# A dense expert layer: 128 instead of 112 tokens scattered through DRAM, 32 instead of 36 lots of one-hot products, another place for two exponentials and for the zeroing of the scratch

## The reference

```python
def peer(h, w_q, sub_keys, u_tab, v_tab):          # h: 256 tokens, width 1024
        q = (xc @ w_q).reshape(T, PEER_HEADS, 2, PEER_QDIM // 2)
        s = jnp.einsum('thcd,hcnd->thcn', q, sub_keys)       # 8 heads x 2 halves x 128 keys
        sv, si = lax.top_k(s, PEER_TOPK)                     # 16 of 128
        comb = (sv[:, :, 0, :, None] + sv[:, :, 1, None, :]).reshape(T, PEER_HEADS, 256)
        cv, ci = lax.top_k(comb, PEER_TOPK)
        eidx = i1 * PEER_NKEYS + i2                          # one of 128 * 128 experts
        w = jax.nn.softmax(cv, axis=-1)
        a = jax.nn.gelu(jnp.einsum('td,thkd->thk', xc, u_tab[eidx])) * w
        return jnp.einsum('thk,thkd->td', a, v_tab[eidx])
```

## Time and profile before

| | |
|---|---|
| median of 3 runs | 2952.64 us (2947.97 to 2952.76) |
| the profiled execution | 2951.89 us, of which the span is 2950.2 us |
| PE busy | 2817.8 us, 96% of the span |
| DVE / ACT / POOL busy | 1989.1 / 1482.9 / 489.1 us |
| chain that ended last | PE 90%, DVE 4%, ACT 3%, DMA 2%, issue 1% |
| granted TensorE clock | 0.982 of full speed on average |
| indirect DMAs (L800) | 256, 420.1 us busy on POOL, mean 1641 ns |

### The profile page before, as it was taken

How to read it: one execution, slowest core, us unless ns; L and a number is a source line. 1 busy time by engine, 2 the same in 40 slices (tenths; PEclk the granted TensorE clock), 3 DMA queues, 4 the chain that set the end, 5 groups by cost and what they waited for, 6 DMA issues and landing times.

```text
span 2950.2 us, 51661 instructions
## 1 busy us (share of the span) xinstructions
PE 2817.8 (96%) x17556; PEld 2517.7 (85%) x17556; DVE 1989.1 (67%) x3725; ACT 1482.9 (50%) x2397; POOL 489.1 (17%) x390
## 2 busy tenths in 40 slices
PE   8889998999999989999999999999899999999998
PEld 6679887788789889999988888785899999988886
DVE  4557975679965759866866666516479848766666
ACT  2444454544443444667855555205245668745554
POOL 0000100011100000477700000000000787400000
PEclk9999999999999999999999999989999999999999
DMA  8638973489854445666556666540355775566663
GB/s 283 209 116 260 346 252 112 128 243 355 331 171 129 143 143 177 176 174 157 137 178 215 214 215 213 126 143 15 93 176 178 178 174 135 145 212 216 215 213 131
DMA packets 355204, 547.85 MB, mean 186 GB/s; under 512 B 71073, under 2 KB 251681, under 8 KB 354466
## 3 DMA queue, kind: packets, MB, share of 16 engines
q1 hardware_dynamic: 303618, 471.46, 50.3%
q0 software_dynamic: 51488, 75.11, 9.8%
HBM read 545.33 MB, written 15.84 MB: 190 GB/s over the span
## 4 chain that ended last, share of the span: by engine, by line
PE 90%; DVE 4%; ACT 3%; DMA 2%; issue 1%; ACTq 0%; SPq 0%; DVEq 0%
PE ps L1002 34%; PE ps L929 12%; PE ps L933 12%; PE ps L930 12%; PE ps L980 4%; PE ps L1369 2%; DMA tile_ring<-mlp_w_in 1%; PE ps L1490 1%; PE ps L904 1%; PE ps L1132 1%; PE ps L863 1%; PE ps L1579 1%; PE ps L874 1%; PE ps L964 1%; PE ps L1030 1%
## 5 line engine op out<-in xcount | busy, mean ns | idle before, releaser
L929 PE MATMUL ps<-x_high,w_high 128*128 128x256 f32 x3264 | 819.2, 288 | 28.5 <-DVE x_low L2730 10.6
L930 PE MATMUL ps<-x_low,w_high 128*128 128x256 f32 x3264 | 805.1, 284 | 0.0
L929 PEld LDWEIGHTS ps<-x_high,w_high 128*128 128x128 f32 x3264 | 628.5, 193 | 41.3 <-issue 26.0
L800 POOL DMA_INDIRECT by_key<-spare x256 | 420.1, 1641 | 1330.3 <-DVE spare L2805 1216.0
L930 PEld LDWEIGHTS ps<-x_low,w_high 128*128 128x128 f32 x3264 | 629.8, 193 | 0.4
L2231 DVE TENSOR_TENSOR w_low<-tile_ring,w_high 128x1024 fp32r<-128x1024 f32 x256 | 313.8, 1226 | 249.4 <-ACT w_high L1821 249.4
L933 PE MATMUL ps<-x_high,w_low 128*128 128x256 f32 x3264 | 460.8, 284 | 1.4 <-DVE w_low L3026 1.4
L1821 ACT ACTIVATE w_high<-tile_ring 128x1024 fp32r<-128x1024 f32 x256 | 271.5, 1061 | 346.0 <-PE ps L1002 346.0
L933 PEld LDWEIGHTS ps<-x_high,w_low 128*128 128x128 f32 x3264 | 423.9, 193 | 1.6 <-DVE w_low L3026 1.6
L1002 PE MATMUL ps<-w_high,x_high 128*128 128x512 f32 x1440 | 389.9, 393 | 21.2 <-DVE x_low L2186 16.7
L1964 ACT ACTIVATE w_high<-tile_ring 128x1024 fp32r<-128x1024 f32 x256 | 270.7, 1058 | 262.9 <-PE ps L933 215.5
(11 more groups left out here) (365 smaller groups left out, 3253.2 us busy)
## 6 DMA issues: line engine op xcount, KB each, us to landing
tile_ring<-peer_u SPq DMA_DIRECT2D x256, 512.0 KB
tile_ring<-peer_v SPq DMA_DIRECT2D x256, 512.0 KB
arena<-mod_w POOLq DMA_DIRECT2D x112, 512.0 KB, 6.4
tile_ring<-mlp_w_in SPq DMA_DIRECT2D x64, 512.0 KB
tile_ring<-mlp_w_out SPq DMA_DIRECT2D x64, 512.0 KB
tile_ring<-ret_w_in SPq DMA_DIRECT2D x48, 512.0 KB
tile_ring<-peer_w_q SPq DMA_DIRECT2D x32, 512.0 KB
by_key<-zero_rows POOLq DMA_DIRECT2D x16, 896.0 KB, 5.1
```

The costliest lines, as they stand in the source:

```text
L800: pool.indirect_dma_start(out=flat, out_offset=bass.IndirectOffsetOnAxis(ap=slot_at[0:SCATTER, n:n + 1], axis=0), in_=slot_weight[0:SCATTE ...
L929: nc.tensor.matmul(dst, cols, x_high[:, c, :], start=c == 0, stop=False)
L930: nc.tensor.matmul(dst, cols, x_low[:, c, :], start=False, stop=False)
```

## The change

- `SCATTER` becomes 128: the whole first block of tokens goes by the indirect DMAs, which then have 128 elements each; the scratch grows from 128 x 128 x 112 to 128 x 128 x 128 floats. The second block goes as 32 lots, after the tiles 92 to 123. Only the second block's routing is turned (three records), and DVE lifts it in one piece.
- The exponentials move from 36 and 68 tiles to 32 and 64, and from between two loops into four pairs that are written out: they now stand behind the first `high` of these four and ahead of its gelu.
- The zeroing of layer 0's scratch moves behind the modulation loads and `ret_const`, and layer 1's behind layer 0's scatters; each has 8 DMAs of 1 MB instead of 896 KB, each waited for as before.
- DVE drops one product of 128 x 128 in the first block's `finish`.

```diff
-SCATTER = 112
+SCATTER = P
-RAISED_AT = (36, 68)
+RAISED_AT = (32, 64)
...
-                        ("cross1", 4), ("mlp1", 16), ("retention", 8), ("gates", 8), ("route0", 18),
-                        ("weigh0", LOTS), ("nsa", 20), ("route1", 18), ("weigh1", LOTS)):
+                        ("cross1", 4), ("mlp1", 16), ("retention", 8), ("gates", 8), ("route0", 17),
+                        ("weigh0", LOTS), ("nsa", 20), ("route1", 17), ("weigh1", LOTS)):
...
-            n_clear = 0
-            for l in range(DEPTH):
-                for i in range(P // CLEAR):
-                    pool.dma_start(by_key[l][:, i * CLEAR:(i + 1) * CLEAR, :],
-                                   I["zero_rows"].rearrange("p (i t) -> p i t", t=SCATTER)).then_inc(cleared, 16)
-                    n_clear += 16
-                    pool.wait_ge(cleared, n_clear)
...
-            landed = 0
+            n_clear, landed = 0, 0
+
+            def clear(l):
+                nonlocal n_clear
+                for i in range(P // CLEAR):
+                    pool.dma_start(by_key[l][:, i * CLEAR:(i + 1) * CLEAR, :],
+                                   I["zero_rows"].rearrange("p (i t) -> p i t", t=SCATTER)).then_inc(cleared, 16)
+                    n_clear += 16
+                    pool.wait_ge(cleared, n_clear)
+            clear(0)
...
+                if l + 1 < DEPTH:
+                    clear(l + 1)
...
-                for b in range(TB):
-                    u = open_unit()
-                    for k in range(3):
-                        mm = nc.tensor.transpose(bank(u)[:, k * P:(k + 1) * P], route[:, b, k, :], ident)
-                    mm.then_inc(unit_done, 1)
+                u = open_unit()
+                for k in range(3):
+                    mm = nc.tensor.transpose(bank(u)[:, k * P:(k + 1) * P], route[:, 1, k, :], ident)
+                mm.then_inc(unit_done, 1)
...
-                def tiles(j):
+                def tiles(j, raise_block=None):
                     for k in range(RING):
                         high(k + 2, j)
+                        if k == 0 and raise_block:
+                            raise_block()
                         gelu(k, j)
...
-                    act.wait_ge(routed, TB * l + b + 1)
-                    A(route[:, b, 2, :], route[:, b, 2, :], ACT.Exp).then_inc(pick_exp, 1)
-                    j0 = RAISED_AT[b] // RING
+
+                    def raise_block():
+                        act.wait_ge(routed, TB * l + b + 1)
+                        A(route[:, b, 2, :], route[:, b, 2, :], ACT.Exp).then_inc(pick_exp, 1)
+                    tiles(RAISED_AT[b] // RING, raise_block)
+                    j0 = RAISED_AT[b] // RING + 1
...
-                    ins = V.tensor_tensor(own, own, wide, ALU.mult)
-                    if b == 1:
-                        operand(ins)
+                    else:
+                        operand(V.tensor_tensor(own, own, wide, ALU.mult))
...
-                    z = bank(u)[:, 0:3 * P].rearrange("p (k t) -> p k t", t=P)[:, :, 0 if i else SCATTER:P]
-                    own = slice(P - SCATTER, own_tokens) if i else slice(0, P - SCATTER)
-                    V.tensor_scalar(minus[:, :, own], z[:, 0:3:2, :], -1.0, None, ALU.mult).then_inc(dve_step, 1)
+                    z = bank(u)[:, 0:3 * P].rearrange("p (k t) -> p k t", t=P)
+                    V.tensor_scalar(minus, z[:, 0:3:2, :], -1.0, None, ALU.mult).then_inc(dve_step, 1)
                     settle()
-                    return V.tensor_copy(slots[:, :, own], z)
-                take(2, lift_slots)
+                    return V.tensor_copy(slots, z)
+                take(1, lift_slots)
```

More of the change, by code:

```diff
@@ L694, in peer @@
                 bare.up(P)
-                units.up(2 + LOTS)
+                units.up(1 + LOTS)
                 panels_next()
```

## The result

The median of six runs is 2963.17 us (2958.1 to 2965.31), against 2950.99 us for the kernel before (six runs, 2947.07 to 2952.76). The ratio is 1.004, 95% interval 1.0027 to 1.0053. The forecast was 2939.7 us; its range ended at 2947.5. The profiled execution has a span of 2963.6 us, 13.4 more than before.

The account below looks back on a forecast made before the run. PE bounds the kernel, with 90% of the chain. Fewer lots -7.1, turned routing -0.7, table loads -6.3, stall +0.9 and zeroing +1.0 give -12.2 us: from 2951.89 to 2939.7 us, range 2935.5 to 2947.5.

Parts of the forecast that it names:

- the scatters' duration: POOL's 256 scatters: 128 elements for 112 add 159 ns each, 20.4 us over a layer's 128, just hidden.
- the rivals with late scatters: Scatters a little late, 2946.1 us, up to 2948, chance 0.12; or slower than the kernel before, chance 0.04.
- the scatters set the end of peer_u: SP's wait: above 0.28 us extra per scatter, two layers lose over 18.1 us, kernel slower by 0.2%; chance 0.04.
- 128e - 26.8: Loss per layer in us where positive, for extra time e per scatter: nothing at 159 ns, 3.2 us at 234.
- The slack: Time before SP needs layer 0's scatters: 22.3 us spare against 20.4 added, with POOL starting at about 1201.5.
- the sum: All terms over the kernel: -7.1 - 0.7 - 6.3 + 0.9 + 1.0 = -12.2 us.
- Lots and turned routing: Peer layers: four fewer lots each gain 7.1 us on PE, three fewer turned records gain 0.7 us.
- Table loads in the loops: ACT's gelu table reloads in later peer_u loop rounds go: 3.17 us a layer, 6.3 us gained.
- The stall at the exponential: PE's wait at each exponential grows by 0.22 us, four times: 0.9 us lost; one distance near 4.8 at each.
- Zeroing: Scratch clearing moved beside tile loads slows products by 1.3%: 1.0 us lost in all, bounds 0 to 6.
- just hidden: Scatters' added 20.4 us a layer fit in 22.3 us of spare time before SP waits, so nothing is lost.

Follow-up runs that it names:

- e1: The changed kernel with 112 instead of 128 elements in each scatter, tokens 112 to 127 getting no weights: 2938.79 us, ratio 0.9964.
- e4: The changed kernel with SCATTER back at 112 (36 lots, six turned records), exponentials and zeroing as changed: 2946.76 us, ratio 0.9986.
- e3: The kernel before with only the exponentials moved, to 32 and 64 tiles in written-out pairs, ahead of gelu: 2948.40 us, ratio 0.9991.
- e7: The changed kernel with the exponentials between the loops as before, at 32 and 64 tiles: 2947.32 us, ratio 0.9989.
- e10: The changed kernel with only the exponential moved behind the first gelu: 2966.35 us, ratio 1.0049.
- e6: The changed kernel with DVE's `w_low` in two instructions of 512 columns: 2940.19 us, ratio 0.9965.
- e5: The kernel before with exponentials at 32 and 64 tiles in written-out pairs, behind the first gelu: 2939.53 us, ratio 0.9964.

## Why the prediction was wrong

**The step that failed** is the scatters' duration: "I take 159, 20.4 us over a layer's 128", with "in proportion 1641 x 16/112 = 234 ns" as upper bound. It measured 264. What failed is not just the size but the form. The mean of 1641 ns was read as a cost of the elements; it was 1.47 us undisturbed, and the rest waiting behind DVE, above all `w_low`, which depends on the phase of two engines. The undisturbed scatter grew by 0.08 us, half of what I took; longer waits, the capture above all, added the rest. So the upper bound, proportion, was none: it had no term for a wait. The hint stood in the earlier trace rows, single scatters between 1.46 and 1.88 us, and I used it only as "for it" of the rivals with late scatters, 0.12 and 0.04. The spread of one instruction's duration wanted an explanation before its mean was scaled.

**The rival that came about** is "the scatters set the end of peer_u". It named the place, SP's wait ahead of its first group; its condition, e above 0.28 us, is not needed, since other things went against the kernel too. Its formula, 128e - 26.8, gives 7.0 us a layer at e = 0.264; measured were 8.52 and 6.48, together 15.0 for 14.0. The slack was read right: POOL began at 1204.92, not 1201.5, but this execution had reached the peer layer 2.8 us later than the one before, which leaves 0.6.

**The other parts.** e1 has all of them and is 12.4 us faster where the sum says 12.2. So close a fit is in part luck: by the profiles its two peer_u stages are 6.45 and 4.93 us shorter, 11.4 where the sum has 13.2, and its zeroing cost peer_v nothing where the sum has 1.0.
- Lots and turned routing: 8.0 us between e4 and e1, forecast 7.8.
- Table loads in the loops: between the exponentials all of layer 0's distances in the changed kernel are 2.88 us, none 3.17; layer 0 in e3 confirms the size. Two table loads a block are left, 1283 ns each.
- The stall at the exponential: 4.85 and 4.87 us in layer 0, forecast near 4.8. ACT of the changed kernel shows the order. The Trainium skill ("ScalarE: Activation LUTs", What ACT_TABLE_LOAD costs) adds some 1.38 us of drain to a load. That drain doesn't show here either: the exponential starts 1.29 us behind the start of its load.

```profile
1201.56 1.28 ACT L2022 ACT_TABLE_LOAD   x1
1202.85 0.31 ACT L2022 ACTIVATE route<-route 128x128 f32<-128x128 f32 x1
1203.18 1.28 ACT L1971 ACT_TABLE_LOAD   x1
1204.48 0.38 ACT L1971 ACTIVATE arena<-ps 128x256 f32<-128x256 f32 x1
```

  In layer 1 it was 5.49 with 3.74 behind it, and 5.54 with 3.69: the granted clock fell there (0.92 from 2270 to 2280 us, 0.83 from 2276 to 2286), 1.5 us each, 3.0 us that the sum lacks. In e1, where it fell at one of the two, layer 1's peer_u stage is 1.5 us longer than layer 0's (414.71 for 413.22).
- Zeroing: forecast 1.0 us, found none. Layer 0's peer_v products took 351.07 us in the changed kernel and 350.05 before, which looks like the forecast. But beside the same zeroing they took 349.96 in e7 and 349.79 in e10. What differs is the clock: over its first 10 us of peer_v PE had 0.72 in the changed kernel, 0.83 before, 0.84 in e7 and 0.86 in e10; 10 us at 0.11 less make about the 1.0 us. It starved no tile.

**What of the total is accounted for.** -12.2 + 15.0 gives +2.8 us; measured are +12.2 by medians and +13.4 by the spans. The two peer_u stages alone were to gain 13.2 us (the sum without the zeroing) and gained 9.9 beside the idle time, 3.0 of the gap being layer 1's clock. Of the 13.4: +2.8 ahead of the first peer layer, +2.1 and +1.0 in layer 0's peer_u and peer_v, +4.2 in the sparse attention between the layers, +3.1 in layer 1's peer_u, +0.3 behind. The two peer_u stages are what the argument covers: the idle time less the gains. The 4.2 us come with another course of the clock: it averages 0.90 from 1880 to 1960 us, before 0.98. In the other kernels' profiles this stage took 297.2 to 298.8 us, as after (298.75), and the 294.6 of the kernel before was the exception. The 2.8 ahead of the peer layer lie inside what the profiles of these kernels scatter by there (it begins at 1089.9 to 1096.7 us; at 1096.7 also in e6's page, a kernel whose median is 23 us lower). Neither is caused by anything the change does there that I can name. So about 7 of the 13.4 us are not explained, and of what lies between the changed kernel and e1, 24.4 us by medians and 26.5 by the spans, only 16.5 lie in the two peer_u stages; 6.1 lie ahead of them, where both run the same instructions. That stays open. It doesn't touch the cause of the loss: e1 removes the loss by the scatters alone, and e6 by `w_low` alone.

## What to carry to other kernels

When an instruction's duration varies in a trace, explain the spread before scaling the mean: here 1.47 of 1.64 us were the instruction's own, even these grew by 0.08 us and not by the 0.21 of proportion, and the rest was waiting for a neighbour's instruction. Where two engines run in loops of almost the same period and one blocks the other, a few hundredths of a microsecond decide whether they fall into step; compare the sum of the blocked round (blocker, tail, gap) with the period, and shorten the blocker if it is longer. A transfer that is "just hidden" with 2 us to spare of 300 should carry more than the 16% that the prediction gave to its being late, all the more when the same change speeds up what hides it.

## What the runs showed of the hardware

- A scatter issued by POOL while DVE runs a subtraction with both inputs in SBUF ends 1.34 us (112 elements) to 1.42 us (128) behind that subtraction's end, whether it began 0.66 or 0.08 us into it: nearly its whole undisturbed length of 1.47 or 1.55. What counts is which began first: of the scatters between 1190 and 1375 us, the 40 of the changed kernel that began inside a `w_low` all ended 1.41 to 1.44 us behind it, and before, of 42 that began ahead of a `w_low` and ran into it, 39 kept their 1.46 to 1.48 us. `w_low` itself is not held by a scatter: 1.21 to 1.25 us with one running, and the same without.
- Not every long DVE instruction holds a scatter. POOL and DVE of the changed kernel:

```profile
1270.95 1.55 POOL L802 DMA_INDIRECT by_key<-spare  x1 [0.30 <-issue]
```

```profile
1270.87 1.21 DVE L2905 TENSOR_REDUCE route<-arena 128x64 f32<-128x1024 uint32 x1
```

  This one, with one input, is as long as `w_low`, and the scatter that began 0.08 us into it kept its 1.55 us; so did one that began 0.25 us into a product with one of its two inputs in PSUM (1496.46). The 15 scatters of layer 0 that began inside another `TENSOR_TENSOR` with both inputs in SBUF were held as by `w_low`, with tails of 1.42 to 1.44 us.
- The Trainium skill ("SBUF — State Buffer", A bandwidth-pool intuition that's wrong) has the same form for a DMA that POOL issues beside a `tensor_copy`, blocked until DVE's end, with about 0.115 us behind it; the tail here is over ten times that. The Trainium skill's box in "SBUF: two separate sides" describes such a copy locking GpSimd out while descriptors are written; that here nearly the whole scatter comes behind `w_low`'s end agrees with it. By the same section an operation with two SBUF inputs locks only against GpSimd operations that read SBUF. The rows above agree as to the two inputs; the scatter's indices and weights lie in SBUF, but no run tells which of its accesses is held up.
- Splitting DVE's 1.23 us into 0.69 and 0.68 us costs DVE 0.06 us a tile (end at 1224.93 for 1224.87) and frees POOL after the first half.
- TensorE's granted clock fell behind an idle time of about 2 us in layer 1 and not behind the same idle time in layer 0 (e3); with 0.36 us of idle time it stayed (e5). It is not the layer that decides: in e6 it fell at layer 0's second exponential too (distances of 5.82 and 3.40 us, 0.83 from 1298 to 1308), and in e1 it stayed at 1.00 at layer 1's second (4.85). What decides is open.
- Zeroing 1 MB at a time beside tile loads, from 1506 to 1556 us, the core moved 327 GB/s and ACT waited for a tile for 0.4 us at most.
